# A third pair of buffers for the experts' down weights, where the residual rows lie

## The reference, cut to what matters

```python
g1, g_idx = lax.top_k(group_probs, 1)                 # one of 4 groups
top_v, top_i = lax.top_k(sel, TOP_K_IN_GROUP)         # two experts inside it
expert_id = g_idx * EXPERTS_PER_GROUP + top_i
combine = jnp.sum(jax.nn.one_hot(expert_id, N_EXPERTS) * (g1 * g2)[..., None], axis=1)
for e in range(N_EXPERTS):
    he = jax.nn.silu(xt @ w_gate[e]) * (xt @ w_up[e])  # 1024 -> 256
    y = y + combine[:, e:e + 1] * (he @ w_down[e])     # 256 -> 1024
...
x = x + y.reshape(B, T, D)
return _rmsnorm(x, final_norm)
```

## Time and profile before

| what | us |
|---|---|
| median of 3 runs (lowest, highest) | 1566.35 (1565.29, 1567.44) |
| the profiled execution, its own time | 1568.13 |
| span of its trace | 1566.3 |
| PE busy | 1488.1 (95% of the span) |
| expert stage: from the first down product to the last instruction of the tail | 1262.5 to 1563 |

### The profile page before, as it was taken

One profiled execution on the slowest core, in us unless ns is written; L12 is line 12 of the kernel. 1 busy time (PEld: TensorE's weight loads), 2 busy tenths in 40 slices (PEclk: granted clock), 3 DMA queues, 4 the chain that ended last, 5 costly groups with the idle time before them and its releaser, 6 DMA issues.

```text
span 1566.3 us, 17162 instructions
## 1 busy us (share of the span) xinstructions
PE 1488.1 (95%) x6625; PEld 776.1 (50%) x6625; DVE 536.0 (34%) x1157; ACT 460.9 (29%) x954; POOL 325.6 (21%) x351
## 2 busy tenths in 40 slices
PE   5998899999999999999999999999999899999987
PEld 2676454444676454444676444454455533333332
DVE  0164410666543230476442201222244531122115
ACT  1232531221855252222764121233232111111112
POOL 1020100444000020356000000014432143343300
PEclk7999999999999999999999999999999899999999
DMA  9556033331030211211010322111602599999985
GB/s 352 197 211 250 1 108 135 107 108 54 1 111 1 97 54 57 78 54 54 1 55 1 108 90 71 54 55 58 243 1 95 194 352 413 408 404 387 412 319 218
DMA packets 85111, 233.76 MB, mean 149 GB/s; under 512 B 16816, under 2 KB 24758, under 8 KB 70824
## 3 DMA queue, kind: packets, MB, share of 16 engines
q1 hardware_dynamic: 69986, 204.00, 34.7%
q0 software_dynamic: 13824, 24.98, 4.4%
q10 hardware_dynamic: 1222, 3.70, 0.6%
HBM read 266.39 MB, written 16.80 MB: 181 GB/s over the span
## 4 chain that ended last, share of the span: by engine, by line
PE 87%; issue 3%; DVE 3%; ACT 3%; DMA 2%; POOL 1%; SPq 0%; POOLq 0%; DVEq 0%; ACTq 0%
PE PS L1875 17%; PE PS L2349 11%; PE PS L2041 9%; PE PS L2107 7%; PE PS L2375 6%; PE PS L1955 5%; PE PS L1852 4%; PE PS L2206 4%; PE PS L2105 4%; PE PS L1977 3%; PE PS L1965 3%; PE PS L2150 2%; PE PS L2177 1%; DMA RING<-in_w_mod_dram 1%; PE PS L2338 1%
## 5 line engine op out<-in xcount | busy, mean ns | idle before, releaser
L1875 PE MATMUL PS<-RH,RING 128*128 128x512 f32 (+1 forms) x864 | 319.0, 527 | 3.4 <-DMA RING<-in_w_in_dram 3.4
L1875 PEld LDWEIGHTS PS<-RH,RING 128*128 128x128 f32 x864 | 164.9, 193 | 148.7 <-issue 135.9
L2041 PE MATMUL PS<-RING,RY 128*128 128x512 f32 x320 | 139.5, 593 | 0.0
L2349 PE MATMUL PS<-RING,RM 128*64 128x512 f32 x384 | 112.7, 593 | 5.5 <-DVE RM L1698 2.9
L1332 DVE SCALAR_TENSOR_TENSOR RM<-RM,COL 128x512 f32<-128x512 f32 (+1 forms) x180 | 114.1, 701 | 0.1
L2107 PE MATMUL PS<-RH,RING 128*128 128x512 f32 x256 | 114.1, 594 | 0.0
L1374 DVE TENSOR_REDUCE SMALL<-PS 128x1 f32<-128x768 f32 (+1 forms) x80 | 67.9, 849 | 128.8 <-PE PS L1955 128.8
L646 POOL TENSOR_SCALAR SMALL<-SMALL 128x1 f32<-128x1 f32 (+1 forms) x32 | 9.9, 310 | 470.4 <-ACT WS L877 227.4
L1955 PE MATMUL PS<-RK,RH 96*128 96x256 f32 (+1 forms) x288 | 105.0, 484 | 1.4 <-ACT WS L1024 1.1
L2041 PEld LDWEIGHTS PS<-RING,RY 128*128 128x128 f32 x320 | 60.1, 190 | 71.1 <-issue 71.1
L648 POOL TENSOR_TENSOR SMALL<-SMALL 128x1 f32<-128x1 f32 (+2 forms) x54 | 56.5, 1046 | 87.3 <-DVE SMALL L1306 84.7
(11 more groups left out here) (370 smaller groups left out, 2205.2 us busy)
## 6 DMA issues: line engine op xcount, KB each, us to landing
RING<-in_w_in_dram SPq DMA_DIRECT2D x18, 2048.0 KB, 8.0
RING<-in_w_mod_dram SPq DMA_DIRECT2D x12, 2048.0 KB, 9.2
RING<-in_w_expert_gate_dram SPq DMA_DIRECT2D x19, 1024.0 KB
RING<-in_w_expert_up_dram SPq DMA_DIRECT2D x19, 1024.0 KB
RING<-in_w_out_dram SPq DMA_DIRECT2D x8, 2048.0 KB, 8.2
RM<-in_w_expert_down_dram SPq DMA_DIRECT2D x16, 1024.0 KB
RK<-in_w_expert_down_dram SPq DMA_DIRECT2D x8, 1024.0 KB
X<-in_w_expert_down_dram SPq DMA_DIRECT2D x8, 1024.0 KB
```

Of the source, the lines that this page charges most:

```text
L1875: last = mm(o[:, 0:T], w[:, k, m * P:(m + 1) * P], HT[:, k, 0:T], start=(k == 0), stop=(k == 7))
L2041: last = mm(PS[:, j % 2, :], YT[:, k, t * P:(t + 1) * P], w[:, k, :], start=(k == 0), stop=(k == 7))
L2349: last = mm(PS[64 * z:64 * z + 64, n % 2, :], XGT[n % 2][:, k, 64 * z:64 * z + 64], free(GU[n % 3][z], [2048, 2], [1, DE], off=DE * k), st ...
```

## The change

The down weights get three sets. The new set 0 lies in `X[:, 2:6]`, the residual rows; the two old sets become 1 and 2. The down weights of pairs 2 and 1 are loaded early, those of pair 0 only after the rows are in DRAM, turned for the router and squared. In the loop SP's waits for down products are one pair looser, and POOL loads the down weights of over pairs one iteration earlier. Behind the down product of pair 21, SP loads the residual rows back from DRAM (four transfers of 512 KB), and `pair_sums` waits for them too.

```diff
-        DN = [[RK[:, 4096:6144], XCTX], [RM[:, 6144:8192], RM[:, 8192:10240]]]
+        XR = [X[:, 2 * z + 2:2 * z + 4, :].rearrange("p a b -> p (a b)") for z in range(2)]
+        DN = [XR, [RK[:, 4096:6144], XCTX], [RM[:, 6144:8192], RM[:, 8192:10240]]]
...
-                        sp.dma_start(DN[n % 2][z], wd[2 * m + z]).then_inc(w_dn[n % 2], 16)
+                        sp.dma_start(DN[n % 3][z], wd[2 * m + z]).then_inc(w_dn[n % 3], 16)
...
+            load_down(2)
+            sp.wait_ge(p_pv2, 16)
             load_down(1)
-            sp.wait_ge(p_pv2, 16)
-            load_down(0)
...
             load_gate_up(1)
+            sp.wait_ge(d_xn, 16 * 4)
+            sp.wait_ge(p_rt, 5)
+            sp.wait_ge(a_ms.sem, a_ms.through(5))
             sp.wait_ge(m_xt, 1)
+            load_down(0)
             sp.dma_start(GU[2][0][:, 2048:4096], wu[first_third]).then_inc(w_gu[2], 16)
...
-                if n - 1 >= 2:
-                    sp.wait_ge(m_dn, 2 * (n - 2))
+                if n - 1 >= 3:
+                    sp.wait_ge(m_dn, 2 * (n - 3))
                     load_down(n - 1)
+            sp.wait_ge(m_dn, 2 * (NP - 3))
+            load_down(NP - 1)
+
             sp.wait_ge(m_dn, 2 * (NP - 2))
-            load_down(NP - 1)
+            for t in range(4):
+                sp.dma_start(X[:, 2 + t, :], xn_d.rearrange("(t p) d -> p t d", p=P)[:, t, :]).then_inc(d_g[t], 16)
...
-                    g.wait_ge(m_dn, 2 * (n - 1))
+                    g.wait_ge(m_dn, 2 * (n - 2))
                     for z in range(2):
-                        over_rows(n, z, DN[n % 2][z], wdr, o_dn[n % 2])
+                        over_rows(n, z, DN[n % 3][z], wdr, o_dn[n % 3])
...
-                if 2 <= n + 1 < NP:
-                    over_down(n + 1)
+                if 3 <= n + 2 < NP:
+                    over_down(n + 2)
...
-                v.wait_ge(d_g[t], 32)
+                v.wait_ge(d_g[t], 48)
...
-                pe.wait_ge((o_dn if TILE_PAIRS[n][0] == "over" else w_dn)[n % 2], 32 * loads_through(n, 2))
+                pe.wait_ge((o_dn if TILE_PAIRS[n][0] == "over" else w_dn)[n % 3], 32 * loads_through(n, 3))
...
-                                      DN[n % 2][z][:, 1024 * j + 512 * c:1024 * j + 512 * c + 512], start=(j == 0), stop=(j == 1))
+                                      DN[n % 3][z][:, 1024 * j + 512 * c:1024 * j + 512 * c + 512], start=(j == 0), stop=(j == 1))
```

More of the change, by code:

```diff
@@ L423, in build @@
         d_fw = sem("final_weight_loaded")
-        o_gu, o_dn = [sem(f"overflow_gate_up_loaded{n}") for n in range(3)], [sem(f"overflow_down_loaded{n}") for n in range(2)]
-        w_gu, w_dn = [sem(f"gate_up_loaded{n}") for n in range(3)], [sem(f"down_loaded{n}") for n in range(2)]
+        o_gu, o_dn = [sem(f"overflow_gate_up_loaded{n}") for n in range(3)], [sem(f"overflow_down_loaded{n}") for n in range(3)]
+        w_gu, w_dn = [sem(f"gate_up_loaded{n}") for n in range(3)], [sem(f"down_loaded{n}") for n in range(3)]
         g_x = [sem(f"rows_gathered{n}") for n in range(4)]
```

## The result

The changed kernel takes **1554.49 us** (median of 4 runs, 1552.66 to 1555.62) against 1565.82 for the kernel before, measured beside it (4 runs, 1564.24 to 1567.44). The ratio is 0.9921, with a 95% interval of 0.9907 to 0.9936: faster by 11.3 us. A second measurement on another chip gave 1555.91 (5 runs) against 1566.05 (9 runs), ratio 0.9937 [0.9923, 0.995]: 10.1 us. The forecast was 8.9 us.

What follows compares the result with a forecast made beforehand. PE's waits for weights were taken to bound the kernel, losing 13.54 us. The terms 4.15 + 4.8 - 0.1 gave 8.9 us, from the median 1566.35 to 1557.4 us; range 1552.5 to 1563.0.

Steps and rivals of the forecast that it cites:

- What bounds the kernel: Stage from pair 1's to pair 21's down product: PE's waits for weights lose 13.54 us, the most to be won.
- Steps 1 and 2: SP's loop transfers go out earlier, gate and up weights by 4.8 us; the 4.15 us around pairs 8 to 10 go.
- step 2: First stall: SP's 4.8 us lead frees pairs 9 and 10, POOL's places free pair 8; all 4.15 us go.
- Step 3: POOL's queue: two places earlier, 5.4 us; wait before down(19) falls to 3.5 us, winning 4.8 of 9.23 us.
- My two ends: Landing of pair 19's down weights: 1491.0 if only two places count, 1486.8 if the 4.15 us lead counts too.
- Step 4: SP's queue at the end: weights of pairs 21 to 23 follow without a gap; otherwise gate_up(23)'s would be late.
- Step 5: Pair 0's down weights, moved later, land near 1250 for a product at 1262.47; cost zero.
- Step 6: Residual rows loaded back behind down(21), covered by the pair rows; VectorE up to 2 us late, taken as 0.1.
- A: Rival: all stage stalls go, 13.5 us won, 1552.8 us; chance 0.24.
- B: Rival: last DMA engine bounds, pair 19's weights land at 1496.35 again, PE waits longer; 1566.4 us; chance 0.12.
- C: Rival: SP's fuller queue starves POOL's, pair 19's weights land 8.3 us later; 1574.7 us; chance 0.06.

Runs made afterwards that it cites:

- experiment 6: The changed kernel with POOL's over_down(n + 2) ahead of gather(n + 5) instead of behind it; 1553.16 us, ratio 0.9924.
- POOL alone: The changed kernel with SP's waits for down products put back as in the kernel before; 1560.96 us, ratio 0.9964.
- SP alone: The changed kernel with POOL's down weights of over pairs put back in their old places; 1560.45 us, ratio 0.9962.
- two sets, one wait gone (3): The kernel before, except that SP no longer waits for down products of over pairs, of which it loads nothing; 1560.66 us, ratio 0.9967.
- two sets, both edits (9): The kernel before, without SP's idle waits for over pairs and with POOL's over_down(n + 1) ahead of gather(n + 5); 1559.49 us, ratio 0.9958.
- late alone (11): The kernel before, with SP's idle waits removed for over pairs 19 and 20 alone; 1567.68 us, ratio 1.0008.
- early alone (12): The kernel before, with SP's idle waits removed for over pairs 4, 5, 8 and 11 alone; 1561.64 us, ratio 0.996.
- experiment 4: The changed kernel with two empty scatters added in POOL's queue just ahead of pair 20's down weights; 1563.99 us, ratio 0.9987.
- experiment 10: The kernel of experiment 6 with residual rows 2 and 3 each loaded just ahead of their own pair rows; 1554.22 us, ratio 0.9917.
- experiment 7: The changed kernel with the four residual row loads moved behind SP's waits for the scatters; 1557.69 us, ratio 0.9947.

## Why the prediction was right, and where it was wrong

**What bounds the kernel: right.** All that could be won by the loads lay in PE's waits for weights, 13.54 us; in the traced execution of experiment 6 the stage loses nothing.

**Steps 1 and 2, SP's earlier transfers and the first stall: right.** Pair 6's gate weights went out 4.80 us earlier in the stage's own time, as worked out, and the 4.15 us round pairs 8 to 10 are gone. The parts show what I had not priced: that stall needs both. POOL alone leaves 2.33 before gate_up(9) (SP's weights), SP alone leaves 2.60 before down(8) (POOL's). The split of step 2, pairs 9 and 10 to SP and pair 8 to POOL, holds.

**Step 3, POOL's places: the step that failed.** I gave pair 19's down weights two places, 5.4 us, left open how much of a lead survives a backlog, and took the middle: a wait of 3.5 us before down(19). It is gone altogether. In the stage's own time (counted from the start of down(0)) its weights were there 1496.35 - 1262.47 = 233.9 us in before. My two ends, 1486.8 and 1491.0, are 224.3 and 228.5 in that time. The profile of two kernels tells when the second of pair 19's down transfers landed. Their DMA issues (what, count, us from issue to landing), first the changed kernel:

```profile
X<-in_w_expert_down_dram,WROW POOLq DMA_INDIRECT x1, 27.0
```

and SP alone:

```profile
X<-in_w_expert_down_dram,WROW POOLq DMA_INDIRECT x1, 9.0
```

Issued at 1453.28 and at 1472.84, they landed at 1480.3 and at 1481.8, or 222.1 and 221.7 us after down(0). (For pair 20 the same view gives 31.8 us from 1463.33, so 1495.1, and PE's wait ends at 1495.25: the two agree.)

So the weights came 11.8 us earlier in the changed kernel, 0.8 us ahead of their product, and not the 5.4 to 9.6 that I had between my ends. But SP alone, with pair 19 in its old places, has them 12.2 us earlier. And POOL alone, with SP's lead gone, has them at least 8.1 us earlier (down(19) starts there at 1486.80, 225.8 us after down(0), without a wait). Each part alone brings most of it, and both together bring no more. A sum of places and a share of the lead, which is what step 3 was, has no room for that.

What it took for granted is the last engine's lag. The wait ends with the last of the 16 engines, and I let that one stay 14 us behind the average. The average can be read: when POOL's queue had done 144 packets for each place up to pair 19's last, 12816 in the old order and 12528 in the new. In before (1235 to 1481.8), in the changed kernel (1230.67 to 1463.5) and with SP alone (1232.66 to 1479.8):

```profile
q0 software_dynamic: 12820, 23.13, 25.8%
...
q0 software_dynamic: 12529, 22.36, 26.7%
...
q0 software_dynamic: 12827, 23.13, 25.9%
```

The same for the others, in us after down(0):

| kernel | the average is through pair 19's places | its last engine is |
|---|---|---|
| before | 219.3 | 233.9 |
| changed | 205.4 | 222.1 |
| POOL alone (1) | 207.6 | 225.8 or earlier |
| SP alone (2) | 219.6 | 221.7 |
| two sets, one wait gone (3) | 223.2 | 229.8 or earlier |
| two sets, both edits (9) | 220.7 | 221.8 |
| late alone (11) | 226.6 | 235.4 |
| early alone (12) | 217.1 | 231.9 |

The last engine doesn't follow the average. In the changed kernel the average is 14 us ahead of before, and the last engine 17 us behind it; with SP alone the average is no earlier at all, and the last engine only 2 us behind. Without that lag there would have been no old wait: in before the average was through at 219.3, and down(19) wanted its weights at 227.1 (1489.53 - 1262.47). The places have the average wrong too. It moved with the time of issue: POOL issued pair 19's down weights 14.2 us earlier in the changed kernel (1451.99 - 1258.14 against 1470.53 - 1262.47), and the average came 13.9 earlier; POOL alone issued them 11.2 earlier (at 1457.80), and the average came 11.7 earlier, where two places are 5.4. With SP alone, SP's queue was nearly dry some 25 to 35 us ahead of the product (three windows of 4 us with 34, 1 and 26 packets, where the driest of before in that part had 69), and a lagging engine may catch up then; but that is argued, since the queue rows add the engines up. What decides the lag stays open. SP's lead isn't needed for POOL's 691 packets in 4 us: POOL alone, with SP's waits those of before, did 685 from 1466 to 1470 us, beside 50 of SP's.

**What was late next.** I had pair 19 stay late, and so didn't ask for the next over pair. It is down(20), with 2.50 and 2.52 us. Its weights are issued at 1462.04, behind the gather of pair 23 (1458.42), which PE wants later. The price of such a place is shown from both sides. One place earlier the wait is gone (experiment 6: landed at 1463.32 + 28.9, 234.0 us after down(0), against 237.0). Two empty places later the weights come 5.4 us later (experiment 4).

The sizes, then: behind the first stall 10.79 - 4.15 = 6.6 us of the stage were won where step 3 had 4.8. With 4.15, and 0.3 in the tail where step 6 had -0.1, that makes 11.1 for 8.9. The 0.3 isn't a gain of the change: the two-set kernels of experiments 3, 9, 11 and 12, whose tail is that of before, have 43.8 to 44.0. That 6.6 came out near 4.8 is in part luck, since the old wait and the new one, of pair 20, both hang on a lag that I had not asked about.

**Step 4, no gap in SP's queue: right.** No wait before any main pair's product in the changed kernel.

**Step 5, down(0) moved at no cost: right.** The stretch took the 2.1 MB at a share of 0.91, counted by the stage's own time (forecast near 0.9), and no product of pairs 0 to 2 waits.

**Step 6, the rows back from DRAM: right here, by its cover.** VectorE's last pair_sums in the changed kernel, in order of time:

```profile
1525.97 8.05 DVE L1735 SCALAR_TENSOR_TENSOR X<-RING,WGT,X 128x1024 f32<-128x1024 f32 x6 [2.96 <-DMA RING<-pair_rows]
...
1535.89 2.60 DVE L1735 SCALAR_TENSOR_TENSOR X<-RING,WGT,X 128x1024 f32<-128x1024 f32 x2
```

1535.89 is 28.86 us after the start of down(21), and so is 1551.01 of before (1551.01 - 1522.15): not late by a tenth. My slack was worked out too small: 16.2 - 10.3 is 5.9 us, not 5, so at the worst 1 us late and not 2. I had named the cover, and the runs show that it is thin. Once down(20) waits no longer, the same rows are worth 1.5 us (experiment 10 against 6), behind the scatter 2.9 us (experiment 7), and in experiment 1, with down weights a period later, the tail is 3.4 us longer. So SP's part of the change also pays for the rows.

**The rivals.** A (all stalls go, 1552.8) came close in the stage: 10.8 of 13.5. B (the last engine is bound by what came before it) fell: pair 19's weights landed at 1480.3, not at 1496.35. The Trainium skill's rule behind it, in "DMA: Bandwidth & Descriptors", Latency and other measured facts, that two of the 16 engines are usually slower, is neither borne out nor refuted: no row names an engine, and what these runs show is a last engine that is 15 us behind the average in one kernel, 17 in another and 2 in a third. C (POOL's queue starves, 1574.7) fell for the change: the average was through pair 19's places 14 us earlier, not later. But what it describes does happen: in experiment 11, where SP's late transfers alone go out earlier, the average got there 7.3 us later than in before, with a new wait before an over pair's gate_up(20). Its last engine lost only 1.5 us. The Trainium skill's rule beside it, in the same page's Queues, rings and completion order, that the engines take turns between queues packet by packet, agrees with the trace: 224 and 223 packets in 4 us where both had work.

**The parts aren't a sum.** By medians POOL alone won 5.2 and SP alone 5.7, together 10.1 to 11.3: that looks like a sum, and is none. In the stage they won 10.5 and 5.9, of 10.8 together; the tail took 3.4 of the first. Half of the gain was to be had without a third set: one wait of SP's, for pairs of which it loads nothing, gave 5.5 us (experiment 3).

## What to carry to other kernels

Look for waits that an issuing engine makes for work that it doesn't load: they hold up everything behind them, and one condition gave half of what a new set of buffers gave here. Price a transfer on a full queue by its place, not its bytes: two empty ones cost 2.7 us each, and the next late consumer is found by asking the same of the pair behind the one just freed. When the last stall on the main engine is gone, look at the tail first, since 2.1 of the last 2.75 us came back there. And where a wait hangs on the last engine of a backlog, don't carry its lag over from one kernel to the next: it moved by more than any term of this sum.

## What the runs showed of the hardware that I had not expected

**A short wait may slow the products behind it, or not.** The same 16 matmuls take 3.58 us in the stream. Behind PE's waits of 2.50, 2.60 and 1.94 us they took 3.65. Behind 2.11, 2.95 and 3.12 us they took 5.35, 5.35 and 5.25, behind 6.48, 6.81 and 7.22 us 5.45, 6.00 and 5.09, and behind 7.06 us 6.53. A wait of 2.11 us cost more than one of 2.60, and 7.22 less than 2.95: length alone doesn't order them. The three dear short ones all stand before down(14), the cheap ones before down(20) and down(8). The granted clock of such stretches in experiment 2, for the two waits of 2.60 and 2.95 us:

```profile
1356.76:1360.41 3.65, 3.65 (x18) 1.58 (x20) 0.00 (x0) 0.60 (x1) 0.00 (x0) 1.00 1.04 417
1429.94:1435.29 5.35, 5.35 (x18) 2.11 (x20) 0.00 (x0) 0.60 (x1) 0.00 (x0) 0.68 1.03 414
```

One at the full clock (2.4 GHz), the other at 0.68 of it, so partly at the lower level of 1.2 GHz. A forecast should give a stall of 2 to 3 us a price of 0.1 or 1.7 us more, not one in between.

**The last DMA engine's lag isn't a constant.** For pair 19 it was 15 us behind the average in the kernel before, 17 in the changed one, and 2 in experiment 2, where the average was no further than in before.

**A queue alone is three times as fast.** POOL's indirect transfers did 691 packets in 4 us beside SP's dry queue (23 packets), against 215 to 223 beside a full one.

**The stretch ahead of the stage varies by 8 us between executions** of identical code (down(0) at 1258.14 and at 1266.34). Its granted clock in the first 400 us was 0.98 in the one and 0.95 in the other; a span alone can't show an edit worth less than that, the two differences can.
